# Attentions of a three-layer block on one core: values as the standing matrix, turned probabilities as the moving one, heads on column halves, no turning of outputs

## The chip, the cores and the metric

The kernel runs on one core of one Trainium2 chip. The metric is the device time of one execution in microseconds, the median of several runs. In the text PE (TensorE) multiplies matrices, DVE (VectorE) and ACT (ScalarE) do element work and read the accumulators, POOL (GpSimd) does element work on SBUF alone, and SP issues the weight loads.

## The reference, cut to what matters

Sequence 512, width 1024, float32. Two layers come first, one with a state-space scan and a differential attention, one with sliding-window attention (16 heads of 64, 2 key-value heads, window 128), then a block in which several attentions run on one projection, followed by memory attention and a feed-forward. What the change touches is how four of the attentions get from scores to outputs:

```python
def sliding_window_attention(q, k, v, sinks, slopes):
    ...
    logits = logits - sl * dist.astype(jnp.float32)
    logits = jnp.where(valid[None, :, None, None], logits, -jnp.inf)
    ...
    p = jax.nn.softmax(jnp.concatenate([logits, sink], axis=-1), axis=-1)[..., :-1]
    out = jnp.einsum('bnkgqs,bnskd->bnqkgd', p.astype(v.dtype), vv)

def odd_layer(h, w_in, b_in, sinks, w_out):
    ...
    return (o * jax.nn.silu(g)) @ w_out

def _stick_breaking(q, k, v):
        ...
        w = jnp.where(strict, jnp.exp(jax.nn.log_sigmoid(z) + suffix), 0.0)
        return jnp.einsum('bhqk,bkhd->bqhd', w.astype(v.dtype), v)

def _nsa_attention(...):
        ...
        return gb[..., 0:1] * o_cmp + gb[..., 1:2] * o_sel + gb[..., 2:3] * o_win

def _hybrid_mixer(...):
    ...
    merged = (g[:, :, 0] * (o_a.reshape(B, S, BRANCH_WIDTH) @ w_up[0]) +
    ...
```

The stick-breaking attention has 4 heads. Beside it stand a top-k attention (4 heads, an index picks 256 of the keys, then softmax and values) and `_nsa_attention` (4 heads; compressed, selected and window keys, each with its own softmax and gate).

Every output then goes, feature by feature, into a matrix product (`w_out`, `w_up`).

## The kernel before

All weights stream from memory: SP loads a 128x1024 piece `raw`, ACT cuts the high part (`cut_hi`, L224), DVE or POOL the low part (`cut_lo`, L229, which engine is set per projection by `low=`), and PE multiplies in three passes, high by high, low by high, high by low (`product`, L241 to L243). PE's order is the program order of the code: each attention is a `Part` with one generator per engine, and between the steps of an attention it takes turns from a "fill", another projection's products, so that PE has work while the softmax runs. A `run(...)` (L250) is a list of parts between two barriers of all engines.

**Sliding and branch attention.** Both are made by `attend_pairs` (L1065). A unit is a pair of heads and a tile of 128 queries; the sliding part has 32 units, the branch part 24. In step i PE computes the scores of unit i (L1139 or L1143), DVE masks them and takes the maximum (a custom instruction, L1263, twice), ACT takes the exponential with the row sums; in step i+2 PE turns the probabilities (transposes, L1166) and ACT copies them to SBUF as `pT` (L1206); in step i+3 PE multiplies (L1156) with `pT` as the standing matrix and 64 columns of values as the moving one, so the output has queries on partitions; DVE then adds the sink to the sum (L1237), takes the reciprocal (L1238), multiplies by the gate (L1240, branch only) and divides the output (L1248, or L1245 where it adds to an earlier one). Before the next unit's values PE waits for that (`out_done`). With windows of 256 keys both heads go in one group of values and one of turns; in the branch part (up to 512 keys) each head has its own.

**Outputs.** Since the next product needs features on partitions, the outputs are turned once more: by `turn_pair` (L2057) in the sliding part and in `LastTurns`, by `Turn` (L797, 24 transposes, with ACT L814 and DVE L826 cutting the high and low parts) ahead of `up`.

**Stick breaking.** For each of 4 heads PE multiplies `sb_p` tiles by values, ten matrix products of 64 columns (L2586), and DVE copies four 128x64 pieces (L2684).

**Selection.** During the branch part DVE also finds the top 256 of each index row by rounds of MAX8 and MATCH_REPLACE8 (L2805, L2807), spread over the first 21 steps (`Selection.span`).

A float32 product appears in the trace as two records, a transpose as one.

## Time and profile before

| what | value |
|---|---|
| median of 3 runs | 1581.39 us (1580.73 to 1582.72) |
| profiled execution | 1585.86 us, its span 1584.0 us |
| PE / DVE / ACT / POOL busy | 1539.8 / 841.3 / 668.0 / 265.5 us |
| sliding part, 566 to 668 us | PE 99.21 of 102 us, DVE 66.71, ACT 75.14, POOL 26.79 |
| stick breaking, 817 to 906 us | PE 88.08 of 89 us |
| branch part, 916 to 1035 us | PE 113.35 of 119 us, DVE 92.00, POOL 39.65 |

Busy times are unions of the engine's records. Records of consecutive matmuls overlap (a record lasts 0.27 to 0.40 us, while the next starts 0.1 to 0.23 us later), so the price of a group of matmuls on PE is read from start to start: from its first record to the first of what follows.

### The profile page before, as it was taken

The numbers are of one execution on the slowest core, as the hardware profiler recorded it, in microseconds if no ns is written. First come the engines' busy times: TensorE is split into PE (matmuls) and PEld (weight loads), VectorE is DVE, ScalarE is ACT, GpSimd is POOL, SyncE is SP. The second block draws the span as 40 slices with busy tenths as digits, with TensorE's granted clock in tenths as the row PEclk, the third lists the DMA queues.
The fourth block names the chain that finished last, engine by engine and source line by source line (L and its number), as shares of the span: only waits on it lengthen the run. The fifth ranks groups of instructions, "written<-read, shape, count | busy, mean of one in ns | idle before, by whom it ended". The sixth has DMA issues, their size and how long they took to land. (4 is left out here: it accounts for less than half of the span.)

```text
span 1584.0 us, 20960 instructions
## 1 busy us (share of the span) xinstructions
PE 1539.8 (97%) x7902; PEld 1272.3 (80%) x7902; DVE 841.3 (53%) x1645; ACT 668.0 (42%) x1390; POOL 265.5 (17%) x170
## 2 busy tenths in 40 slices
PE   8999999999999999998999999899999999999997
PEld 7888878888787889887888777778877888888886
DVE  3222289957834566536624476847655444444224
ACT  4222356565523367624235454553255232232122
POOL 0001044255400013200012232322322000000000
PEclk9999999999999999999999999999999999999999
DMA  5226356311322431123431211312311322322322
GB/s 213 95 94 175 104 145 162 94 47 48 120 94 80 141 92 41 42 93 97 146 96 65 80 54 54 108 41 94 103 71 41 107 93 93 107 93 94 105 94 80
DMA packets 47459, 150.21 MB, mean 95 GB/s; under 512 B 6464, under 2 KB 6848, under 8 KB 47232
## 3 DMA queue, kind: packets, MB, share of 16 engines
q1 hardware_dynamic: 41664, 136.34, 26.9%
q10 hardware_dynamic: 5696, 12.55, 2.5%
q8 instruction: 63, 1.03, 0.3%
q14 instruction: 36, 0.29, 0.1%
HBM read 128.02 MB, written 2.10 MB: 82 GB/s over the span
## 5 line engine op out<-in xcount | busy, mean ns | idle before, releaser
L224 ACT ACTIVATE cut_hi<-raw 128x1024 fp32r<-128x1024 f32 x228 | 241.5, 1059 | 561.2 <-PE ps L241 557.1
L241 PE MATMUL ps<-h_hi,cut_hi 128*128 128x512 f32 (+1 forms) x1120 | 447.8, 400 | 3.7 <-DVE h_lo L449 1.1
L243 PE MATMUL ps<-h_hi,cut_lo 128*128 128x512 f32 (+1 forms) x1120 | 436.5, 390 | 0.0
L242 PE MATMUL ps<-h_lo,cut_hi 128*128 128x512 f32 (+1 forms) x1120 | 436.1, 389 | 0.0
L229 DVE TENSOR_TENSOR cut_lo<-raw,cut_hi 128x1024 fp32r<-128x1024 f32 x170 | 211.8, 1246 | 397.2 <-ACT cut_hi L224 397.2
L241 PEld LDWEIGHTS ps<-h_hi,cut_hi 128*128 128x128 f32 x1120 | 211.3, 189 | 54.7 <-issue 13.3
L243 PEld LDWEIGHTS ps<-h_hi,cut_lo 128*128 128x128 f32 x1120 | 210.9, 188 | 45.0
L242 PEld LDWEIGHTS ps<-h_lo,cut_hi 128*128 128x128 f32 x1120 | 211.6, 189 | 37.5
L229 POOL TENSOR_TENSOR cut_lo<-raw,cut_hi 128x1024 fp32r<-128x1024 f32 x56 | 135.3, 2417 | 469.4 <-ACT cut_hi L224 469.4
L241 PE MATMUL ps<-cut_hi,h_hi 128*128 128x512 f32 (+1 forms) x304 | 117.6, 387 | 3.4 <-DVE cut_lo L229 2.9
L243 PE MATMUL ps<-cut_hi,h_lo 128*128 128x512 f32 (+1 forms) x304 | 116.7, 384 | 0.0
L242 PE MATMUL ps<-cut_lo,h_hi 128*128 128x512 f32 (+1 forms) x304 | 116.6, 384 | 0.0
L1156 PEld LDWEIGHTS ps<-arena,scr 128*128 128x128 f32 x464 | 62.5, 191 | 11.7 <-issue 4.5
L241 PEld LDWEIGHTS ps<-cut_hi,h_hi 128*128 128x128 f32 x304 | 57.1, 188 | 16.2 <-DVE cut_lo L229 3.4
L241 PE MATMUL ps<-cut_hi,ff_hi 128*128 128x512 f32 x176 | 68.6, 390 | 0.1
L242 PE MATMUL ps<-cut_lo,ff_hi 128*128 128x512 f32 x176 | 68.5, 389 | 0.0
L243 PE MATMUL ps<-cut_hi,ff_lo 128*128 128x512 f32 x176 | 68.5, 389 | 0.0
L243 PEld LDWEIGHTS ps<-cut_hi,h_lo 128*128 128x128 f32 x304 | 57.1, 188 | 11.4
L242 PEld LDWEIGHTS ps<-cut_lo,h_hi 128*128 128x128 f32 x304 | 57.1, 188 | 11.1
L1156 PE MATMUL ps<-arena,scr 128*128 128x64 f32 x464 | 61.5, 268 | 3.5 <-DVE arena L1245 1.9
L2226 POOL TENSOR_TENSOR small<-small 128x1 f32<-128x1 f32 x4 | 2.2, 548 | 360.8 <-DVE small L2238 360.8
L1206 ACT ACTIVATE scr<-scr,small 128x256 f32<-128x256 f32 (+3 forms) x112 | 56.8, 508 | 0.0
(366 smaller groups left out, 2285.2 us busy)
## 6 DMA issues: line engine op xcount, KB each, us to landing
raw<-weights SPq DMA_DIRECT2D x228, 512.0 KB, 3.3
tiles_r<-tiles_r SPq DMA_DIRECT2D x96, 128.0 KB, 2.3
scr<-scr ACTq DMA_DIRECT2D x34, 64.0 KB, 3.5
x<-x_in SPq DMA_DIRECT2D x4, 512.0 KB, 6.5
x<-x_in ACTq DMA_DIRECT2D x1, 2048.0 KB, 8.4
q_stack<-qT_lo ACTq DMA_DIRECT2D x16, 128.0 KB, 2.3
out<-x SPq DMA_DIRECT2D x4, 512.0 KB, 2.6
consts<-tables ACTq DMA_DIRECT2D x1, 1732.0 KB, 8.0
```

The costliest lines, as they stand in the source:

```text
L224: act.activation(cut_hi[:, u % CUT, :], raw[:, u % RAW, :], ACT.Copy).then_inc(hi_ready, 1)
L229: eng.tensor_tensor(cut_lo[:, u % CUT, :], raw[:, u % RAW, :], cut_hi[:, u % CUT, :].bitcast(F32), ALU.subtract).then_inc(lo_ready, 1)
L241: a = pe.matmul(out, left[0], right[0], start=start, stop=False)
L242: pe.matmul(out, left[0], right[1], start=False, stop=False)
L243: return a, pe.matmul(out, left[1], right[0], start=False, stop=stop)
L1156: last = pe.matmul(ps[:, 5, m * 64:m * 64 + 64], pT(m)[:, b * P:(b + 1) * P], u["v"][b][m], start=b == 0, stop=b == nb - 1)
L1206: last = act.activation(prob(i, m), score(i, m) if whole else prob(i, m), ACT.Exp, bias=stat(NMAX, i, m), scale=1.0 if whole else -1.0, ac ...
L2226: pool.tensor_tensor(rs[:, 32 + t:33 + t], ms[:, 32 + t:33 + t], neg_half[:, 0:1], ALU.pow)\
```

## The change

It rewrites four attentions so that the values stand on PE and the turned probabilities move past them, 128 queries at a time. A value matrix has 64 columns, so a head fills one half of the output partitions (`HALVES`), and the two heads of a pair write the two halves of one accumulator bank. The output then already has features on partitions.

- Sliding part (`SlidingWindow` in place of `attend_pairs`): the division moves ahead of the turn, as two DVE multiplications of SBUF probabilities per unit; PE's turns wait for it (`weighed`) instead of the exponential. The sink is a further column of the scores (a 128x2 DVE copy per unit), so ACT's own sink exponentials and L1237 go. `turn_pair` goes; a pair's bank is 2 or 5, and the gates of six pairs come six fill turns earlier in the plan. Two banks for turns, two `pT` buffers.
- Stick breaking: four products per head, 512, 384, 256 and 128 columns wide, and one 64x512 copy.
- Branch part (`Branches`): one group of values per unit, taken before the turns; the division and the gate in one DVE instruction per head; the two gated branches accumulate on PE, and ACT copies each finished bank (4 copies) to `o_f`. Units run by head pair, then tile, then branch. `Selection.span` is 19.
- Compressed keys: two products of 512 columns in place of four of 256. The cuts of `o_abc` (6 on ACT, 6 on DVE) stand here. The part `Turn` goes, with its 24 transposes, and `up` starts the next block.

```diff
-        class Turn(Part):
...
-                        last = pe.transpose(ps[:, k, t * P:(t + 1) * P], self.src(t, k), ident)
-                    last.then_inc(self.turned, 1)
...
-        def attend_pairs(tag, units, width, fill=None, lead=None, rest=None):
...
-                            if step >= LAG:
-                                i, u = step - LAG, units[step - LAG]
-                                nb = len(u["v"])
-                                pe.wait_ge(pT_out, ng * i + g + 1)
-                                if g == 0 and i:
-                                    pe.wait_ge(out_done, i)
-                                for m in heads_g:
-                                    for b in range(nb):
-                                        last = pe.matmul(ps[:, 5, m * 64:m * 64 + 64], pT(m)[:, b * P:(b + 1) * P],
-                                                         u["v"][b][m], start=b == 0, stop=b == nb - 1)
-                                last.then_inc(valued, 1)
-                            if 2 <= step < n + 2:
-                                i, u = step - 2, units[step - 2]
-                                pe.wait_ge(expd, i + 1)
...
-                            dve.wait_ge(expd, i + 1)
...
-                            dve.wait_ge(valued, ng * i + ng)
...
-        def turn_pair(pe, k, turned):
-            for t in range(NT):
-                last = pe.transpose(ps[:, 6 + (k + 1) % 2, t * P:(t + 1) * P], o_tok[:, t, k * P:(k + 1) * P], ident)
-            last.then_inc(turned, 1)
+        def pair_bank(k):
+            return (2, 5)[k % 2]
...
-            dve.scalar_tensor_tensor(gT[:, k, :], ps[:, 6 + (k + 1) % 2, :], 0.5, gT[:, k, :], ALU.mult, ALU.mult)\
+            dve.scalar_tensor_tensor(gT[:, k, :], ps[:, pair_bank(k), :], 0.5, gT[:, k, :], ALU.mult, ALU.mult)\
...
+        class SlidingWindow(Part):
...
+                    if step >= self.LAG:
+                        self.value(pe, step - self.LAG)
+                    if 2 <= step < self.n + 2:
+                        i = step - 2
+                        pe.wait_ge(self.weighed, i + 1)
+                        if i >= 2:
+                            pe.wait_ge(self.pT_out, i - 1)
+                        for m in range(2):
+                            for b in range(self.width(i) // P):
+                                at_t = (2 * m + b) * P
+                                last = pe.transpose(self.turn_bank(i)[:, at_t:at_t + P], self.prob(i, m)[:, b * P:(b + 1) * P],
+                                                    ident)
+                        last.then_inc(self.turned, 1)
+                    for _ in range(self.pe_turns(step, 1)):
...
+            def value(self, pe, i):
...
+                for b in range(nb):
+                    for m, r in enumerate(HALVES):
+                        at_t = (2 * m + b) * P
+                        last = pe.matmul(ps[r, pair_bank(k), t * P:(t + 1) * P], v_tok[:, first + b, kv:kv + 64],
+                                         self.pT(i)[:, at_t:at_t + P], start=b == 0, stop=b == nb - 1)
+                last.then_inc(self.valued, 1)
...
+                        dve.tensor_copy(self.sinks_beside(i), neg_sink[:, h:h + 2].unsqueeze(2))
...
+                    if 1 <= step <= self.n:
+                        i = step - 1
+                        dve.wait_ge(self.expd, i + 1)
+                        dve.reciprocal(self.stats(self.RDEN, i), self.stats(self.DEN, i)).then_inc(self.chain, 1)
+                        dve.wait_ge(self.chain, i + 1)
+                        for m in range(2):
+                            p = self.prob(i, m)[:, 0:self.width(i)]
+                            last = dve.tensor_scalar(p, p, self.stat(self.RDEN, i, m), None, ALU.mult)
...
-                if b == 4:
-                    for k in (6, 7):
-                        turn_pair(pe, k, oc_turned)
...
-                    for t in range(NT):
-                        for b in range(t + 1):
-                            last = pe.matmul(sb_out_bank(h, t), sb_p[:, b, t * P:(t + 1) * P],
-                                             tv[:, b, h * 64:(h + 1) * 64], start=b == 0, stop=b == t)
-                        last.then_inc(sb_o, 1)
+                    for b in range(NT):
+                        last = pe.matmul(sb_out_bank(h)[:, b * P:], tv[:, b, h * 64:(h + 1) * 64], sb_p[:, b, b * P:S],
+                                         start=b == 0, stop=b == NT - 1, skip_group_check=True)
+                    last.then_inc(sb_o, 1)
...
-                    for t in range(NT):
-                        dve.wait_ge(sb_o, 4 * h + 4)
-                        dve.tensor_copy(o_abc[:, t, h * 64:(h + 1) * 64], sb_out_bank(h, t)).then_inc(sb_out, 1)
+                    dve.wait_ge(sb_o, h + 1)
+                    dve.tensor_copy(o_f[HALVES[h % 2], h // 2, :], sb_out_bank(h)).then_inc(sb_out, 1)
...
-            span = 21
+            span = 19
+            banks = (0, 1, 2, 4, 5, 3)
...
+        class Branches(Part):
...
+                for b in range(nb):
+                    for m, r in enumerate(HALVES):
+                        last = pe.matmul(ps[r, 5, token_of(u)], u["v"][b], self.pT(m)[:, b * P:(b + 1) * P],
+                                         start=u["starts"] and b == 0, stop=u["stops"] and b == nb - 1, skip_group_check=True)
+                last.then_inc(self.valued, 1)
...
+                    if step - self.LAG in self.last_of:
+                        act.wait_ge(self.valued, step - self.LAG + 1)
+                        act.activation(o_f[:, units[step - self.LAG]["tile"], :], ps[:, 5, :], ACT.Copy)\
+                           .then_inc(self.drained, 1)
...
+                                last = dve.tensor_scalar(p, p, r, u["gate"][m], ALU.mult, ALU.mult)
...
+        def branch_low(dve, k):
+            dve.wait_ge(o_high, k + 1)
+            dve.tensor_tensor(o_parts[1][:, k, :], o_f[:, k, :], o_parts[0][:, k, :].bitcast(F32), ALU.subtract)\
+               .then_inc(o_low, 1)
...
-                for t in range(NT):
-                    last = pe.matmul(ps[:, 2 + t // 2, t % 2 * 256:(t % 2 + 1) * 256],
-                                     cs_turned_p[:, t * P:(t + 1) * P], vc_diag, start=True, stop=True)
-                    if t % 2:
-                        last.then_inc(cs_valued, 1)
+                for i in range(2):
+                    pe.matmul(ps[:, 2 + i, :], vc_diag[:, i * P:(i + 1) * P], cs_turned_p, start=True, stop=True)\
+                      .then_inc(cs_valued, 1)
...
+                for k in range(6):
+                    branch_low(dve, k)
...
-        run(turn_o, up, out_m, norm_q, first_query, memory, norm_f, FeedForward(),
+        run(up, out_m, norm_q, first_query, memory, norm_f, FeedForward(),
```

PE in the sliding part, two steps of it; L1139 and L1923 are scores, L1166 and L1938 turns, L1156 and L1956 values, L2057 the output turns. Before:

```order
L1139 MATMUL ps<-k_his,q_stack 128x256
L1139 MATMUL ps<-k_los,q_stack 128x256
L1139 MATMUL ps<-k_his,q_stack 128x256
L1139 MATMUL ps<-k_los,q_stack 128x256
L2057 MATMUL ps<-consts,arena 128x128 x4
L241 MATMUL ps<-h_hi,cut_hi 128x512
L242 MATMUL ps<-h_lo,cut_hi 128x512
L243 MATMUL ps<-h_hi,cut_lo 128x512
L1156 MATMUL ps<-arena,scr 128x64 x2
```

After:

```order
L1923 MATMUL ps<-k_his,q_stack 128x256
L1923 MATMUL ps<-k_los,q_stack 128x256
L1923 MATMUL ps<-k_his,q_stack 128x256
L1923 MATMUL ps<-k_los,q_stack 128x256
L241 MATMUL ps<-h_hi,cut_hi 128x512
L242 MATMUL ps<-h_lo,cut_hi 128x512
L243 MATMUL ps<-h_hi,cut_lo 128x512
L1956 MATMUL ps<-scr,arena 64x128 x2
```

The output turns are gone and nothing stands in their place; the value products keep their number and place, with the operands exchanged.

DVE in the sliding part, one step; L1263 and L2006 are the masks and maxima, L694 the fill's. Before:

```order
L1263 ISA scr,small<-ps,consts,small 128x256
L1263 ISA small 128x1
L1263 ISA scr,small<-ps,consts,small 128x256
L1263 ISA small 128x1
L694 TENSOR_SCALAR arena<-ps,cols 128x512
L1237 TENSOR_TENSOR small<-small 128x2
L1238 RECIPROCAL small<-small 128x2
L1248 TENSOR_TENSOR arena<-ps,small 128x128
```

After:

```order
L2003 COPY scr<-small 128x2
L2006 ISA scr,small<-ps,consts,small 128x256
L2006 ISA small 128x1
L2006 ISA scr,small<-ps,consts,small 128x256
L2006 ISA small 128x1
L694 TENSOR_SCALAR arena<-ps,cols 128x512
L2018 RECIPROCAL small<-small 128x2
L2022 TENSOR_SCALAR scr<-scr,small 128x128 x2
```

The division no longer reads PE's output; it works on probabilities in SBUF, and the reciprocal belongs to the unit before rather than to the one four before.

PE in the branch part where three-block units meet four-block ones; L1143 and L2871 are scores, L1166 and L2884 turns, L1156 and L2901 values, L2847 and L2711 belong to the fill. Before:

```order
L1156 MATMUL ps<-arena,scr 128x64 x3
L1166 MATMUL ps<-consts,scr 128x128 x4
L1156 MATMUL ps<-arena,scr 128x64 x3
L1166 MATMUL ps<-consts,scr 128x128 x4
L1143 MATMUL ps<-arena 128x128 x2
```

After:

```order
L2871 MATMUL ps<-arena 128x256 x2
L241 MATMUL ps<-h_hi,cut_hi 128x512
L242 MATMUL ps<-h_lo,cut_hi 128x512
L243 MATMUL ps<-h_hi,cut_lo 128x512
L2711 MATMUL ps<-consts,arena 128x32 x2
L241 MATMUL ps<-h_hi,cut_hi 128x512
L242 MATMUL ps<-h_lo,cut_hi 128x512
L243 MATMUL ps<-h_hi,cut_lo 128x512
L2901 MATMUL ps<-scr,arena 64x128 x8
L2884 MATMUL ps<-consts,scr 128x128 x4
```

Two short value groups per unit have become one of both heads, and fill products stand between the two heads' turns.

## Rows read from the trace of the kernel before

**Rows 1.** The page's first section: busy time, share, instructions by engine.
```profile
PE 1539.8 (97%) x7902; PEld 1272.3 (80%) x7902; DVE 841.3 (53%) x1645; ACT 668.0 (42%) x1390; POOL 265.5 (17%) x170
```
**Rows 2.** Windows: stretch, length, busy by engine, PE clock, DMA share, GB/s.
```profile
566.00:668.00 102.00, 99.21 (x685) 89.42 (x683) 66.71 (x250) 75.14 (x257) 26.79 (x14) 1.00 0.17 50
...
916.00:1035.00 119.00, 113.35 (x789) 88.57 (x789) 92.00 (x297) 63.42 (x155) 39.65 (x18) 1.00 0.23 76
```
**Rows 3.** Windows around the end of the sliding part, same columns.
```profile
660.00:680.00 20.00, 18.61 (x96) 15.50 (x95) 7.36 (x16) 6.58 (x13) 3.80 (x3) 0.91 0.15 52
```
**Rows 4.** PE timeline, sliding: start, duration, engine, line, operation, count, [idle before].
```profile
603.69 1.00 PE L1156 MATMUL ps<-arena,scr 128*128 128x64 f32 x8
604.53 0.61 PE L1166 MATMUL ps<-consts,scr 128*128 128x128 f32 x4
```
**Rows 5.** PE timeline, branch part: a group of four value records.
```profile
1041.72 0.55 PE L1156 MATMUL ps<-arena,scr 128*128 128x64 f32 x4
1042.11 0.39 PE L1166 MATMUL ps<-consts,scr 128*128 128x128 f32 x2
```
**Rows 6.** PE timeline, memory attention: turns, values in halves, scores.
```profile
1187.37 0.66 PE L3337 MATMUL ps<-consts,scr 128*128 128x128 f32 x4 [0.40 <-POOL scr L3389]
1187.96 0.66 PE L3348 MATMUL ps<-scr,arena 128*64 128x128 f32 x8
1188.55 0.70 PE L3324 MATMUL ps<-arena 64*128 64x256 f32 x4
```
**Rows 7.** PE timeline, sliding: one output turn and the products behind it.
```profile
596.73 0.60 PE L2057 MATMUL ps<-consts,arena 128*128 128x128 f32 x4
597.09 0.48 PE L241 MATMUL ps<-h_hi,cut_hi 128*128 128x512 f32 x1
597.40 0.39 PE L242 MATMUL ps<-h_lo,cut_hi 128*128 128x512 f32 x1
597.63 0.40 PE L243 MATMUL ps<-h_hi,cut_lo 128*128 128x512 f32 x1
```
**Rows 8.** PE timeline, stick breaking: one head's values, then one head's scores.
```profile
848.30 2.34 PE L2586 MATMUL ps<-arena 128*128 128x64 f32 x20
850.45 0.48 PE L241 MATMUL ps<-h_hi,cut_hi 128*128 128x512 f32 x1
...
856.11 2.42 PE L2561 MATMUL ps<-arena 64*128 64x512 f32 x8
858.46 0.66 PE L2564 MATMUL ps<-masks 128*128 128x128 f32 x4
```
**Rows 9.** PE timeline at the barrier behind the sliding part.
```profile
667.96 0.47 PE L241 MATMUL ps<-cut_hi,yc_hi 128*128 128x512 f32 x1 [1.39 <-PEq L250]
```
**Rows 10.** DVE groups, sliding part (busy, mean ns); then DVE and POOL timeline.
```profile
L1237 DVE TENSOR_TENSOR small<-small 128x2 f32<-128x2 f32 x32 | 11.6, 362 | 0.0
L1248 DVE TENSOR_TENSOR arena<-ps,small 128x128 f32<-128x128 f32 x32 | 9.3, 291 | 9.1 <-PE ps L1156 8.2 <-DVE small L1238 0.3
...
580.14 1.83 DVE L1237 TENSOR_TENSOR small<-small 128x2 f32<-128x2 f32 x1
...
579.58 2.38 POOL L229 TENSOR_TENSOR cut_lo<-raw,cut_hi 128x1024 fp32r<-128x1024 f32 x1 [8.84 <-ACT cut_hi L224]
```
**Rows 11.** DVE groups by form, branch part, 916 to 1036 us: busy, mean ns.
```profile
L1240 DVE TENSOR_TENSOR small<-small,arena 128x2 f32<-128x2 f32 x16 | 6.5, 407 | 0.5
...
L2811 DVE TENSOR_SCALAR arena<-arena 128x256 f32<-128x256 f32 x1 | 0.3, 293 | 0.0
```
**Rows 12.** DVE, then PE timeline where the compressed keys end and `up` begins.
```profile
1083.15 1.23 DVE L229 TENSOR_TENSOR cut_lo<-raw,cut_hi 128x1024 fp32r<-128x1024 f32 x1 [0.58 <-ACT cut_hi L224]
...
1086.79 1.88 DVE L826 SCALAR_TENSOR_TENSOR o_abc_lo<-ps,o_abc_hi 128x512 fp32r<-128x512 f32 x3 [1.62 <-ACT o_abc_hi L814]
...
1085.50 2.81 PE L797 MATMUL ps<-consts,arena 128*128 128x128 f32 x24 [0.78 <-PEq L250]
1088.13 0.51 PE L241 MATMUL ps<-o_abc_hi,cut_hi 128*128 128x512 f32 x1
```

More of the change, by code:

```diff
@@ L3068, in act @@
                 act.activation(cs_turned_p, ps[:, 4, :], ACT.Copy).then_inc(cs_pT, 1)
+                next(filler)
+                for k in range(4):
+                    branch_high(act, k)
+                for i in range(2):
+                    act.wait_ge(cs_out, i + 1)
+                    branch_high(act, 4 + i)
                 for _ in filler:
```

568 lines of the change are left out of this document (282 added, 286 removed).

## The prediction

> **What bounds the kernel now.** I read the page's busy line first: PE works 1539.8 us of a span of 1584.0, twice as long as DVE and more than twice as long as ACT [rows 1]. So time is won or lost on PE, and elsewhere only where PE comes to wait. Next the windows over the two large attentions: the sliding part has PE busy in 99.21 of its 102 us, with DVE at 66.71 and POOL at 26.79; the branch part has PE at 113.35 of 119, DVE at 92.00, POOL at 39.65 [rows 2]. The branch part is thus the one place where a second engine is near. Last the timelines of PE, in which a group's price is read from its first record to the first of the next kind. The sum below is made against the profiled execution, 1585.86 us with a span of 1584.0; the median of the runs is 1581.39, 4.5 lower, and I carry the difference over to it.
>
> **Value groups of the sliding part.** Eight old value records run from 603.69 to 604.53, 0.84 us [rows 4]; four take 0.39 [rows 5]; so a record adds about 0.11. The new form stands in the memory attention already: eight records, alternating between the two column halves, take 0.59 from 1187.96 to 1188.55. The last of them starts about 0.375 after the first (duration of the group 0.66 less one record of about 0.285). If they start in pairs, one per half, that is three steps of 0.125 per pair, where two old records take 0.22. But the neighbours pay: the four turns ahead of them take 0.59 [rows 6], where four turns among full-size tiles take 0.36 [rows 7]. Part of these 0.23 belongs to the change from the scores' tile before, so I charge half, 0.12, to entering the half-width tiles. A new group then costs 0.71 with four pairs, 0.46 with two, 0.96 with six and 1.21 with eight, an estimate. The sliding part has 8 units of one block (0.39 to 0.46) and 24 of two (0.84 to 0.71): 24 x 0.13 less 8 x 0.07, **2.5 us won**.
>
> **Value groups of the branch part.** Each unit has two old groups, one per head: at 0.11 a record, 0.17, 0.39, 0.61 and 0.84 for 1 to 4 blocks, twice 2.01 = 4.02 over the four widths. The new single groups cost 0.46 + 0.71 + 0.96 + 1.21 = 3.34. Six sets of four widths: **4.1 us won**. Over both parts that is 47.4 us of old groups against 40.8, with 232 pairs. The nearest rows below are pairs that run one record behind the other, 0.22 a pair; above, pairs at the pitch of one old record, 0.11 or a little less. I take 0.125, from the one row with this operation.
>
> The Trainium skill speaks of this swap: "TensorEngine Tiling (Array Packing)", section "Theoretical Speedup", gives up to 2x where the small dimension is at most 64. By that the 47.4 us would fall to 23.7; our row with its switches gives 40.8 (the rival "full halving" below carries its own working).
>
> **Output turns.** One `turn_pair` takes 0.36 from 596.73 to 597.09, and the product after it starts 0.31 ahead of the next, rather than 0.23: 0.44 together [rows 7]. Six go from the sliding part, **2.6 us**. The eight in `LastTurns` go as one group, 2 x 0.36 + 0.08 = **0.8 us**. Nothing takes their place in PE's order.
>
> **Stick breaking.** A head's 20 records take 2.15, from 848.30 to 850.45. The new form has eight records of 512 to 128 columns, of which only one column half works at a time. The nearest row is the same head's scores, the same eight widths: 2.35, from 856.11 to 858.46 [rows 8]. With 0.08 for the entry that is 2.43, 0.28 more, four times: **1.1 us lost**. Fewer DVE copies help nobody here.
>
> **Barrier behind the sliding part.** PE waits 1.39 there [rows 9], since DVE divides the last output and then does a bias, before the barrier. Now nothing of the attention follows the last values, and the bias can be done before. Some 0.5 of the gap stays; **0.9 won**.
>
> **Join at `up`.** The 24 transposes from 1085.50 to 1088.13 vanish, but not their time. DVE has finished the additions 0.58 before 1083.15, at 1082.57; now six cuts of 1.88/3 = 0.63 follow, 3.8, then `cut_lo`, 1.23, which makes 1087.6, then the last copy and the barrier; in the trace `cut_lo` ends at 1084.38 and PE starts 1.12 later, of which 0.37 or so is a wait [rows 12]. So `up` starts at 1088.3 to 1088.7 instead of 1088.13: **0.4 lost**. PE's own cover is gone: it idles for over 3 us, where it now turns.
>
> **The clock.** The gap of 1.39 at 667.96 is followed by a granted clock of 0.91 over 20 us [rows 3], some of these at the lower level of 1.2 GHz: 20 x 0.09 = 1.8 us. The gap at the join grows from 0.78 to over 3 and may be followed by such a stretch, 1.8 lost; the gap behind the sliding part shrinks and may give back as much. I take **0.9 lost**, with bounds of 1.8 either way.
>
> **DVE in the sliding part.** Removed are L1237, 11.6 us, and L1248, 9.3 [rows 10]. Added are two multiplications per unit, which I price with a one-input operation of 256 columns, 0.29 [rows 11], and a small copy of some 0.2: 32 x 0.78 = 25. So 66.7 becomes 70.8. There is a hidden price: at 580.14 a 128x2 addition took 1.83 us, exactly while POOL ran a `cut_lo` that started at 579.58 and took 2.38; the mean of all 32 is 0.36 [rows 10]. If every us of POOL blocked DVE, it would stand at 97.6, just what PE needs after its gain. So the sliding part does not become slower than before, and I leave this at nothing. The new wait of PE's turns on `weighed` lies a step behind the exponentials; queued behind it are that step's fill and next scores, which hide up to about a step's half.
>
> The Trainium skill bears on this too: "SBUF — State Buffer", section "Who interferes with whom", describes the ports that DVE and GpSimd share as an exclusive lock, which copies and tensor-scalar operations take in their fast modes. The new operations are of these kinds, so by that rule the change moves DVE towards the stall; the 1.83 us agrees with there being one, for an addition. The rival "DVE held" has its price from rows.
>
> **DVE in the branch part.** 92.0 now; L1240's 6.5 go [rows 11], L1245 and L1248 go too and are left uncounted; 2 x 0.29 come for each of the 19 units beside which the top-k rounds now have to finish (21 before): 11.0. That is 96.5, against 119 less PE's gain, 115. POOL is busy in a third of this time [rows 2]; a multiplication that meets its 2.4 us loses half of it on the mean, 0.4 a unit, 7.6 in all: 104, still below PE. I leave it at nothing.
>
> **Sum.** 2.5 + 4.1 + 2.6 + 0.8 - 1.1 + 0.9 - 0.4 - 0.9 = 8.5 us. The span goes from 1584.0 to 1575.5, the median from 1581.39 to **1572.9 us**.
>
> **The rivals.**
> *Full halving.* If a pair cost half of two old records with no switches, 47.4 us would become 23.7, and the gain would be 8.5 + 23.7 - 6.6 = 25.6: 1555.8 us. Against it stand the 0.59 of the turns and the 0.59 of the eight records [rows 6].
> *Branch and sliding value gains eaten by DVE's chain.* The division now lies between exponential and turn, and the rounds are pressed into 19 steps, 21/19 as many per step. If PE waits for `weighed` as long as it saves on values, 6.6 us go: 1579.5. For it speaks that DVE has only 27 us left in the branch part, against it that DVE is at most 104 of 115.
> *DVE held by POOL (slower).* If DVE is blocked for all of POOL's 39.65 x 19/21 = 36 us in the branch part, it needs 96.5 + 36 = 132 us against 115: 17 lost, 1590. It begins to cost at 18.5 us of blocking, about half of POOL's time, and eats the whole change at 27. For it: the 1.83 us above. Against it: only the multiplications that arrive during a cut are hit, and two of them stand together.
> *Pairs that do not overlap (slower).* If records of the two halves start one after the other in these places, a pair costs 0.22 instead of 0.125: 232 x 0.095 = 22 us more, 1594.9. The change breaks even at 0.125 + 8.5/232 = 0.16 a pair. Against it: 0.66 for eight records in the memory attention [rows 6], where 0.84 and more would stand.
>
> **How the numbers follow.** Forecast 0.64, with a range of its own: pairs at 0.105 give 232 x 0.02 = 4.6 more, the clock 2.7 more, so 1565.6; downwards pairs at 0.14 cost 3.5, the clock 0.9, some stalls 1: 1578. Full halving 0.06, gains eaten 0.15, DVE held 0.10, no overlap 0.05. A measurement of this kernel tells some 0.2%, 3.2 us, from no change, so 1578.2 and 1584.6 are the borders. Faster: forecast and full halving, 0.70. Same: gains eaten and a fifth of DVE held, 0.17. Slower: the rest of DVE held and no overlap, 0.13. The range goes from 1564 to 1585: full halving, no overlap and most of DVE held stay out, under 0.2.
>
> **What would show it.** In the trace after: a group of eight value records in the sliding part takes about 0.6 to its successor, and the turns behind it no more than before; in the branch part the sixteen-record group takes 1.2 or less. At the end of the sliding part PE's gap is below 0.6. At the join PE idles for 3 us or more and `up` starts no earlier than before. PE's waits in the branch part name DVE for few us; if they name DVE's multiplications for over 8 us, or single multiplications last 1 to 2 us beside POOL's cuts, DVE is held. If value records are spaced 0.1 each, pairs do not overlap. A granted clock below 0.95 in the branch part would mean gaps that I did not count.

## The result: slower by 0.2% instead of faster by 0.5%

The changed kernel takes 1585.9 us (median of 20 runs, 1582.41 to 1589.19) against 1582.19 for the kernel before beside it. The ratio is 1.0021 with an interval of 1.0014 to 1.0028: slower by about 3.3 us, where 8.5 us less were forecast. Its profiled execution has a span of 1587.3 us, against 1584.0; it is the slowest of the twenty (1589.19 us).

Lined up by the first products of each stage, the two traces differ here (us; forecast of the same places beside it). The first row holds nothing that was changed; over the twenty profiles of this case it lies between 507.0 and 511.0, which is how far single executions differ there.

| stage | before | after | difference | forecast |
|---|---|---|---|---|
| start to the fill's products ahead of the sliding part | 511.0 | 509.8 | -1.2 | 0 |
| sliding part, to the first product of `out_c` | 156.9 | 154.8 | -2.1 | -6.0 |
| `out_c` and the normalization behind it | 57.0 | 55.5 | -1.5 | -0.8 |
| projection, stick breaking, branch part to the products behind the compressed blocks | 288.2 | 289.7 | +1.5 | about -2 |
| rest of the branch part, to the memory's projection | 63.9 | 68.1 | +4.2 | about -1 |
| memory's projection and join | 11.16 | 11.14 | 0.0 | +0.4 |
| `up` | 33.4 | 35.9 | +2.5 | +0.9 (clock) |
| all behind | 462.5 | 462.4 | -0.1 | 0 |

The page of after, busy line by engine: PE works 7 us less than before [rows 1], while the span is 3.3 longer. DVE has 29.5 us more.

```profile
PE 1532.7 (97%) x7794; PEld 1233.2 (78%) x7794; DVE 870.8 (55%) x1665; ACT 660.4 (42%) x1322; POOL 266.6 (17%) x170
```

So the work did become cheaper on PE, and the groups show it. PE timeline of after: start, duration, line, count, first in the sliding part (it answers rows 4 and 6), then one head of stick breaking (rows 8), then the longest group of the branch part.

```profile
598.78 0.66 PE L1956 MATMUL ps<-scr,arena 128*64 128x128 f32 x8
599.37 0.66 PE L1938 MATMUL ps<-consts,scr 128*128 128x128 f32 x4
...
843.60 2.37 PE L2451 MATMUL ps<-arena 128*64 128x512 f32 x8
845.89 0.50 PE L241 MATMUL ps<-h_hi,cut_hi 128*128 128x512 f32 x1
...
1043.08 1.09 PE L2901 MATMUL ps<-scr,arena 128*64 128x128 f32 x16
1044.11 0.33 PE L2884 MATMUL ps<-consts,scr 128*128 128x128 f32 x1
```

Eight records take 0.59 to their successor instead of 0.84, sixteen take 1.03, a head of stick breaking 2.29 instead of 2.15. What came in is waits. PE's waits of after, in the sliding part and then from 910 to 1062, and last the longest row of before in this part (who waits, for whom, us in total, times, longest). The second list has 12.9 us in all; before it had 6.6, and the first had 1.3 for DVE:

```profile
PE ps L1938 <- DVE scr L2022: 4.8, 5, 1.6
...
PE ps L2884 <- ACT scr L2917: 7.4, 9, 1.1
PE ps L2901 <- ACT scr L2917: 1.7, 3, 0.7
PE ps L2716 <- DVE small L2729: 1.5, 1, 1.5
PE ps L241 <- POOL cut_lo L229: 1.1, 2, 0.9
PE ps L2884 <- DVE scr L2958: 0.7, 1, 0.7
PE ps L2901 <- ACT arena L2927: 0.5, 1, 0.5
...
PE ps L1166 <- ACT scr L1196: 3.2, 7, 0.7
```

So PE's waits of turns for ACT's copies of the turn bank have grown from 3.2 us to 7.4.

And the clock. Windows of after around the end of the branch part and the join (columns as in rows 2; the eighth is PE's granted clock):

```profile
1050.00:1060.00 10.00, 7.50 (x50) 5.14 (x48) 2.71 (x7) 3.75 (x9) 0.00 (x0) 0.84 0.09 36
1060.00:1070.00 10.00, 9.31 (x65) 8.52 (x66) 2.58 (x6) 4.70 (x9) 0.00 (x0) 0.50 0.01 2
1070.00:1080.00 10.00, 9.33 (x74) 8.89 (x73) 8.20 (x17) 5.42 (x11) 0.00 (x0) 0.98 0.26 81
1080.00:1090.00 10.00, 6.59 (x40) 5.27 (x39) 7.46 (x12) 5.12 (x8) 0.00 (x0) 0.88 0.26 92
1090.00:1100.00 10.00, 10.00 (x37) 8.03 (x35) 5.34 (x7) 1.10 (x2) 0.00 (x0) 0.78 0.26 91
```

From 1060 to 1070 PE ran at 1.2 GHz throughout. Full speed less the granted clock, times the length, is 1.6 + 5.0 + 0.2 + 1.2 + 2.2 = 10.2 us in these fifty; before, the same fifty were at 1.00. Not all of it is time, since PE also waits there: the two stages in which it lies grew by 4.2 and 2.5 us. That is still the largest single item, and the forecast had 0.9 for it, at the join alone.

The mean granted clock of every execution is on record. Over the twenty of the changed kernel it is 0.987 to 0.993, with a median of 0.990 (0.987 in the profiled one); over the 108 executions of the kernel before that were timed beside the experiments it is 0.991 to 0.998, with a median of 0.994. So the lower clock is no accident of the profiled execution, though its size there is at the upper end. At the same mean clock, 0.992, seven executions of the changed kernel take 1584.0 us on the mean and fourteen of the kernel before 1585.0. By this estimate the change would have won about 1 us at an equal clock: the clock makes a loss of it, and waits have eaten most of the gain that was forecast.

### The profile page after: what moved, and what is told of

It reads as the page before. It is cut to its first block and busy times, and to the rows that moved or that the text cites. A ratio compares the mean times of both kernels' runs of the same rounds, so it can differ in the third digit from the quotient of the medians.

```text
span 1587.3 us, 20505 instructions
## 1 busy us (share of the span) xinstructions
PE 1532.7 (97%) x7794; PEld 1233.2 (78%) x7794; DVE 870.8 (55%) x1665; ACT 660.4 (42%) x1322; POOL 266.6 (17%) x170
## 5 line engine op out<-in xcount | busy, mean ns | idle before, releaser
L3500 ACT ACTIVATE scr<-scr 128x512 f32<-128x512 f32 x22 | 13.9, 632 | 101.2 <-DVE scr L3515 101.1
L917 ACT ACTIVATE scr<-scr,small 128x128 f32<-128x128 f32 (+3 forms) x64 | 35.4, 555 | 36.0 <-DVE small L982 36.0
L1058 POOL TENSOR_TENSOR tiles_r<-arena,tiles_r 128x512 fp32r<-128x512 f32 x16 | 21.3, 1352 | 142.1 <-ACT tiles_r L1053 142.1
```

The costliest lines, as they stand in the source:

```text
L917: last = act.activation(prob(i, m), score(i, m) if whole else prob(i, m), ACT.Exp, bias=stat(NMAX, i, m), scale=1.0 if whole else -1.0, ac ...
L1058: pool.tensor_tensor(tiles_r[:, at_lo, :], whole[:, h, :], tiles_r[:, hi, :].bitcast(F32), ALU.subtract)\
L3500: act.activation(silu_of[:, j % 3, :], silu_of[:, j % 3, :], ACT.Silu).then_inc(self.silu, 1)
```

## Experiments

Each kernel was timed beside the kernel before on the same chip; the ratio to it stands with its 95% interval. All start from the changed kernel (ratio 1.0021) unless the text says otherwise.

### Which half: one part alone

The diff was applied in two halves: the sliding part with what belongs to it, or all the rest.

> The kernel before with the sliding part alone rewritten (with the gates and LastTurns that belong to it); stick breaking, branch part and compressed keys as before. Lining up the two traces, the rewritten sliding part lost 2.2 us of length and the product after it 1.4. Theory A (each part moves the time by its own length): 1582.2 - 3.6 = 1578.6 us, PE waiting 4 to 5 us for the multiplications of DVE in the sliding part. Rival B (the parts interact, or the lined-up difference is scatter of one execution): within 1 us of the kernel before.

> The complement: the sliding part as before, stick breaking, branch part, compressed keys and the missing turn as changed. Theory A: the whole loss sits here, 1585.9 + 3.6 = 1589.5 us, with the granted clock at half behind the end of the branch part and behind the join. Rival B (no single part is slow): between 1582 and 1586.

Measured: 1579.19 us, ratio 0.9984 (0.9975 to 0.9994), and 1589.12 us, 1.0045 (1.0033 to 1.0058). The times of theory A came in both, and in the first kernel's trace PE waits 4.8 us for the multiplications. The parts add up (-0.16% + 0.45% = 0.29%, against 0.21%), so the loss sits in stick breaking, the branch part and the join.

What theory A said of the clock did not come. The second kernel's profiled execution (1587.39 us, with a median of 1589.12) has no low clock at the end of the branch part and a short one at the join (0.93 and 0.90 from 1080 to 1100). So the two executions can be compared. PE timeline: the same value group at the end of the part in the changed kernel and in this one; then windows of this one, and one of the kernel before:

```profile
1056.68 1.46 PE L2901 MATMUL ps<-scr,arena 128*64 128x128 f32 x12 [0.58 <-ACT scr L2917]
...
1059.92 0.88 PE L2977 MATMUL ps<-scr,arena 128*64 128x128 f32 x12 [0.58 <-ACT scr L2993]
...
1050.00:1060.00 10.00, 8.28 (x47) 5.30 (x48) 4.41 (x12) 4.71 (x14) 2.52 (x3) 1.00 0.17 54
1060.00:1070.00 10.00, 7.51 (x89) 6.47 (x90) 3.48 (x9) 6.34 (x14) 0.00 (x0) 1.00 0.00 0
...
1060.00:1070.00 10.00, 8.98 (x91) 8.38 (x91) 5.44 (x13) 6.18 (x14) 0.00 (x0) 1.00 0.01 2
```

The gaps of the end are the same five (3.2 us in both kernels). But from the products behind the compressed blocks to the memory's projection this kernel takes 63.9 us, as much as the kernel before, and the changed one 68.1. So what this stage lost is the low clock; the gaps by themselves cost what the cheaper value groups gave. Eight profiled kernels leave the end of the branch part without further work on PE and with one turn bank; seven of them show a granted clock of 0.60 or less over some 10 us there, and this one does not. What decides between them no run shows.

### The clock: work that nobody needs

In the first kernel six transposes of the identity stand behind each head's turns in the two steps of the branch part that have no fill; in the second 24 stand at the end of the compressed keys.

```diff
+                        if step in (self.n, self.n + 1):
+                            for j in range(6):
+                                pe.transpose(ps[:, 0, j % 4 * P:(j % 4 + 1) * P], ident, ident)
```

```diff
+                for i in range(24):
+                    pe.transpose(ps[:, 4, i % 4 * P:(i % 4 + 1) * P], ident, ident)
```

> The changed kernel with six needless transposes behind each head's turn in the two steps of the branch part that have no fill products (24 transposes in all, about 2.6 us of PE work that nothing reads). Theory clock (PE's gaps in the tail let the granted clock fall to half from 1058 to 1070): the clock stays at 1.00 there and, though work is added, the time falls by 4 to 7 us, to 1579 to 1582. Rival chain (the tail is long because turns wait for ACT's copies, and the clock is a side effect without weight): no gain, 1585.9 to 1588.5.

> The changed kernel with 24 needless transposes at the end of the compressed keys, where PE is idle for 3.4 us before the barrier. Theory clock: up starts at the same moment but at full clock, 2 to 2.5 us faster, 1583.4 to 1584. Rival: the clock behind the join stays low because of the tail before it, or the transposes delay the barrier: 1585.9 to 1587.

Measured: 1584.82 us, 1.0014 (1.0005 to 1.0023), and 1582.52 us, 1.0002 (0.9993 to 1.0011). The second is the plain case: added work, and some 3 us won (0.19%). In its trace `up` starts after a gap of 0.78 instead of 3.41, and the clock behind it is at 1.00. PE timeline at the join of after, then of the kernel with the 24, then windows of the latter:

```profile
1089.00 0.76 PE L241 MATMUL ps<-o_abc_hi,cut_hi 128*128 128x512 f32 x1 [3.41 <-PEq L250]
1089.56 0.63 PE L242 MATMUL ps<-o_abc_lo,cut_hi 128*128 128x512 f32 x1
```

```profile
1084.35 2.79 PE L3086 MATMUL ps<-consts 128*128 128x128 f32 x24 
1087.92 0.47 PE L241 MATMUL ps<-o_abc_hi,cut_hi 128*128 128x512 f32 x1 [0.78 <-PEq L250]
...
1080.00:1090.00 10.00, 9.22 (x61) 7.74 (x60) 7.47 (x11) 4.08 (x6) 0.00 (x0) 1.00 0.33 107
1090.00:1100.00 10.00, 10.00 (x46) 8.28 (x45) 6.68 (x10) 1.66 (x2) 3.03 (x3) 1.00 0.32 106
```

A product lasts 0.63 at the lower level and 0.39 at the upper one. The first kernel missed its expectation. Its trace has the clock at 1.00 from 1050 to 1080, and the stage from the products behind the compressed blocks to the memory's projection takes 65.6 us instead of 68.1. The needless work costs nothing at that place: from the value group behind the first gap to the end of the part it is 7.5 us, as in the kernel with the sliding part as before, without transposes and at the same clock. But low stretches stand elsewhere in this execution, 0.94 and 0.89 from 1010 to 1030 and 0.68 from 1080 to 1090, where the changed kernel has 1.00 and 0.88.

### The end of the branch part and the join: useful work in the gaps

```diff
-                return min(step, self.n) * self.fill.pe_turns // self.n
+                return min(step, self.n + 2) * self.fill.pe_turns // (self.n + 2)
```

> The changed kernel with the fill products of the branch part spread over 26 steps instead of 24, so that the two steps without scores have some 10 turns of products (6 to 7 us of useful PE work). Theory tail (the end of the branch part has nothing but dependent turns, copies and values; PE's gaps there cost 3.2 us themselves and let the clock fall): the waits behind 1053 vanish, the clock stays at 1.00, and the time falls by 4 to 7 us to 1579 to 1582. Rival (DVE's rounds bound the first 19 steps, so that products taken from them open waits there): 1585 to 1588, with more PE waits before 1030.

Measured: 1578.87 us, 0.9985 (0.9976 to 0.9994): 0.36%, some 6 us, for one line, as the theory had it. Windows of this kernel:

```profile
1050.00:1060.00 10.00, 9.31 (x91) 7.58 (x90) 1.66 (x3) 3.71 (x6) 2.51 (x3) 1.00 0.17 54
1060.00:1070.00 10.00, 8.46 (x68) 7.89 (x66) 9.72 (x20) 4.87 (x11) 0.00 (x0) 1.00 0.15 52
```

From the projection ahead of stick breaking to the memory's projection its trace takes 353.1 us, the changed kernel 357.8 (289.7 + 68.1), and 353.6 with the end at full clock (289.7 + 63.9). So most of what the line gives is the clock. The waits did not all vanish: turns and values still wait 8.7 us for ACT's copies in the branch part (9.1 in the changed kernel), and the 352.0 us of the kernel before are not reached.

For the join, four `branch_high` moved to the start of the compressed keys on ACT, and three `branch_low` into gaps of DVE:

```diff
+                act.wait_ge(other_attentions.drained, 4)
+                for k in range(4):
+                    branch_high(act, k)
                 norm_kv.high(act)
...
                 next(filler)
+                for k in range(2):
+                    branch_low(dve, k)
                 next(filler)
+                branch_low(dve, 2)
...
-                for k in range(6):
+                for k in range(3, 6):
                     branch_low(dve, k)
```

> The changed kernel with four of the six high cuts of the attention outputs at the start of the compressed keys and three of the low cuts in gaps of DVE, so that three instead of six stand between the last addition and the barrier. Theory join (up waits for DVE's six cuts, and the gap lets the clock fall): PE's gap shrinks from 3.4 to 1.5 us, up starts 1.9 us earlier and at full or nearly full clock, together 2 to 4 us, 1582 to 1584. Rival (the cuts delay the chain of the compressed keys by as much): 1585.9.

Measured: 1580.52 us, 0.9994 (0.9984 to 1.0003), some 4 us, a little more than expected: the stage of memory's projection and join takes 9.3 us instead of 11.1, and `up` 33.4 instead of 35.9, at full clock.

> The changed kernel with both edits that moved the time most: fill spread over 26 steps in the branch part, and the cuts ahead of up begun earlier. Theory (two separate places, each with its own gap and its own stretch at half clock): the gains add, 1585.9 - 7.0 - 5.4 = 1573.5 us. Rival (both gains are largely the same stretch of low clock): 1577 to 1579.

Measured: 1578.24 us, 0.9977 (0.9966 to 0.9988). The sum of the two gains would be a ratio of 0.9958, known to about 0.0015 by the intervals, so the gains added only in part, at the edge of the noise. In part they were the same: with the fill alone, `up` already took 34.7 us instead of 35.9. Both places kept their gain in this kernel's profile, the join 9.3 us and `up` 33.3; but the clock is at 0.83 from 1060 to 1070, so a stretch of it was still lost there.

### The sliding part: held multiplications

Three of the four waits over 0.3 us look alike. DVE, then POOL timeline of after at one of them, then PE; last the same three for the fourth wait, the longest:

```profile
602.91 3.47 DVE L2022 TENSOR_SCALAR scr<-scr,small 128x128 f32<-128x128 f32 x2
...
602.68 2.41 POOL L229 TENSOR_TENSOR cut_lo<-raw,cut_hi 128x1024 fp32r<-128x1024 f32 x1 [7.48 <-ACT cut_hi L224]
605.03 1.27 POOL L1848 TENSOR_TENSOR yc_lo<-arena,yc_hi 128x512 fp32r<-128x512 f32 x1
...
606.44 0.44 PE L1938 MATMUL ps<-consts,scr 128*128 128x128 f32 x2 [0.93 <-DVE scr L2022]
...
567.54 1.97 DVE L2003 COPY scr<-small 128x2 f32<-128x2 f32 x1
...
567.09 2.39 POOL L229 TENSOR_TENSOR cut_lo<-raw,cut_hi 128x1024 fp32r<-128x1024 f32 x1 [60.09 <-ACT cut_hi L224]
...
570.96 0.44 PE L1938 MATMUL ps<-consts,scr 128*128 128x128 f32 x2 [1.63 <-DVE scr L2022]
```

Two multiplications that take 0.27 each elsewhere span 3.47 us, from just after the start of POOL's cut to the end of its second operation, each held by one of the two. In the fourth case no multiplication was held but the copy of the sinks, and all that follows it in DVE's order, the multiplications too, came late. The Trainium skill says as much in "SBUF — State Buffer", section "Who interferes with whom": copies and tensor-scalar operations in their two-port modes contend with GpSimd, and whoever comes second is blocked for the whole instruction of the first. The trace agrees, for the multiplications and for the 128x2 copies (1.97 us at 567.54, 0.16 in the median).

In the first kernel the fill's cuts go to DVE (`low="pool"` left out, POOL's `cut_low` taken away); in the second the turns follow a step later, and with them the fill is spread over one step more:

> The changed kernel with the fill's eight low cuts of the sliding part on DVE instead of POOL, 8 x 1.25 = 10 us more work for DVE, 19 us less for POOL. Theory lock (DVE's multiplications are held while POOL runs a cut, and PE's turns wait for them): PE's 4.8 us of waits for the multiplications fall below 1.5, no multiplication lasts over 1.4 us except beside the six small POOL operations, 1582 to 1583.5. Rival load (DVE simply has too much to do between exponential and turn): the waits grow with the 10 us, 1587 to 1591.

```diff
-            n, LAG, RING, WIDE = SW_H // 2 * NT, 3, 4, 264
+            n, LAG, RING, WIDE = SW_H // 2 * NT, 4, 4, 264
...
-                    if 2 <= step < self.n + 2:
-                        i = step - 2
+                    if 3 <= step < self.n + 3:
+                        i = step - 3
```

> The changed kernel with the turns of the sliding part one step later (three steps behind the scores instead of two, the values four), so that a multiplication of DVE that is held beside a cut of POOL has a step of slack before PE needs it. Theory slack (DVE has time enough on the mean; single multiplications held for 1 to 2 us hit PE because the turn follows too closely): PE's 4.8 us of waits for the multiplications fall below 1, the part gets 3 to 4 us shorter less about 1 for the longer end, 1582.5 to 1584. Rival (DVE is late all along): the waits stay above 3 us, 1585.9 or more.

Measured: 1587.17 us, 1.0041 (1.0027 to 1.0055), and 1581.88 us, 0.9995 (0.9984 to 1.0007). Without POOL's cuts the multiplications are indeed free: their time falls from 29.2 us to 20.7, one of 64 is over 0.7 us. But PE waits 7.0 us for them, since DVE now waits itself, 9.2 us in all, for ACT's high cuts in front of them. DVE groups of that kernel in the sliding part (busy, mean ns, idle before):

```profile
L2021 DVE TENSOR_SCALAR scr<-scr,small 128x256 f32<-128x256 f32 x48 | 15.4, 363 | 0.9
L229 DVE TENSOR_TENSOR cut_lo<-raw,cut_hi 128x1024 fp32r<-128x1024 f32 x9 | 11.0, 1225 | 9.2 <-ACT cut_hi L224 9.2
```

A step of slack does it: with the turns a step later PE's waits for the multiplications are gone, though these take 32.5 us there, more than the 29.2. The sliding part takes 151.1 us, 3.7 less than in the changed kernel and 5.8 less than before, where the forecast had 6.0. So it was one held instruction at a time that came too late, not DVE's load.

### The branch part: who holds the copies

PE's longest row of waits there is the second head's turns for ACT's copy of the first's. One of them, PE and then ACT:

```profile
975.74 0.30 PE L2884 MATMUL ps<-consts,scr 128*128 128x128 f32 x1 [1.06 <-ACT scr L2917]
...
972.94 1.06 ACT L224 ACTIVATE cut_hi<-raw 128x1024 fp32r<-128x1024 f32 x1 [3.49 <-PE ps L241]
973.91 0.58 ACT L672 ACTIVATE arena<-ps 128x512 f32<-128x512 f32 x1
974.38 1.05 ACT L2781 ACTIVATE block_hi<-arena 128x1024 fp32r<-128x1024 f32 x1
975.33 0.27 ACT L2917 ACTIVATE scr<-ps 128x128 f32<-128x128 f32 x1
```

Four edits were made around it: the odd fill turn of a step between the two heads' turns (`k // 2 if half == 0 else (k + 1) // 2`); the division on ACT as a scaled copy, DVE keeping the reciprocal; a bank of its own for the first head's turns; and, on top of that, ACT's fill pieces of a step behind its copies and exponentials.

> The changed kernel with the odd fill turn of a branch step put between the two heads' turns instead of ahead of the values. Theory cover (before, the second head's value group stood between the two turn groups and hid ACT's copy of the single turn bank; now the second turn waits for it, 7.4 us in 9 places, 3 of them in the tail): the waits of L2884 for ACT fall to 2 to 4 us, the time by 2 to 4 us, 1582 to 1584. Rival (the wait only moves ahead of the values, which need both copies of the step before, or DVE sets the pace): within 1 us of 1585.9.

Measured: 1583.42 us, 1.0016 (1.0005 to 1.0027), an interval that overlaps the changed kernel's. The first 18 steps take 103.7 us, as before and as in the changed kernel (103.9), and the waits of turns for copies 5.8 us, with 1.6 us of new ones for DVE's multiplications. The median lies in the theory's range, but neither the ratio (0.8 us less), nor the steps, nor the waits do: the rival.

> The changed kernel with the division of the branch part's probabilities on ACT (two scaled copies per unit) instead of DVE, which keeps the reciprocal and for gated units a 128x2 multiplication: some 22 us less for DVE, 18 to 20 more for ACT. In the trace the first 18 steps take 103.7 to 103.9 us whether before, after, or with fill between the turns. Theory pace (DVE's rounds and multiplications set that pace, and took the gain of the values): these steps take 99 to 101 us, the time falls by 3 to 5 us, 1581 to 1583. Rival (the chain over ACT's copies sets it): the steps take 104 or more, with longer waits of the turns for ACT, 1586 to 1590.

Measured: 1588.49 us, 1.0047 (1.0032 to 1.0062), 106.0 us for the 18 steps, and 7.8 us of waits of turns for ACT. The rival: more load on ACT makes it worse. That DVE set no pace before isn't shown by this, since ACT got what DVE lost; but PE's waits of after name DVE's multiplications here for 0.7 us only.

```diff
+            def turn_bank(self, i, m):
+                return ps[:, 4 if m else (i + 1) % 2 * 2, :]
...
+                        if i >= 3:
+                            pe.wait_ge(self.pT_out, 2 * i - 5)
...
-                        if m == 0:
+                        if m == 1:
                             for _ in range(self.pe_turns(step, 1)):
```

> The changed kernel with a bank of its own for the first head's turns in the branch part (the score bank of the unit after, free by then), so that the second head's turns no longer wait for ACT's copy of the first; the fill turns that stood between the two go behind both. Theory one bank: PE's 7.4 us of waits of turns for ACT's copies fall below 2, the first 18 steps take 100 to 101 us instead of 103.9, the time falls by 3 to 5 us, 1581 to 1583. Rival (the wait moves to the next scores or values, since the chain turn, copy, value itself is too long): the steps stay at 103 to 104 and the time within 1.5 us of 1585.9.

Measured: 1583.39 us, 1.0002 (0.9993 to 1.0012), some 3 us less, but not by the way that the theory named. The waits only moved from the turns to the scores:

```profile
PE ps L2876 <- ACT scr L2924: 6.2, 8, 1.1
PE ps L2716 <- DVE small L2729: 4.3, 1, 4.3
```

The first 18 steps take 102.8 us. Its profiled execution has the clock at 1.00 from 1030 to 1080 (though at 0.70 from 1020 to 1030), so the gain is more likely the end of the part than its pace; this is argued, not shown.

```diff
-                    for _ in range(self.turns(step)):
-                        next(filler, None)
                     for m in range(2):
                         if 2 <= step < self.n + 2:
...
+                    for _ in range(self.turns(step)):
+                        next(filler, None)
                     if step - self.LAG in self.last_of:
```

> The kernel with the bank of its own for the first head's turns (1583.4), in which ACT takes the fill's pieces of a branch step behind the step's copies and exponentials instead of ahead of them. Theory ACT's queue: PE's 6.2 us of waits of the scores for ACT's copies fall below 2, the first 18 steps take 99 to 101 us instead of 102.8, the time falls by 3 to 5 us, to 1578.5 to 1580.5. Rival (the chain of turn, copy and value is too long in itself, or the later cuts make PE wait for weights instead): the waits change their name and the time stays within 1.5 us of 1583.4.

Measured: 1587.56 us, 1.0035 (1.0024 to 1.0047). PE's waits in the branch part:

```profile
PE ps L241 <- POOL cut_lo L229: 9.9, 3, 4.9
PE ps L241 <- issue: 2.2, 1, 2.2
PE ps L241 <- ACT arena L2722: 2.2, 1, 2.2
...
PE ps L2876 <- ACT scr L2922: 0.3, 1, 0.3
```

The waits for copies are gone (0.3 us), so ACT's order is what makes them; but the same order brings the weights late, and PE waits 9.9 us for these. ACT's queue holds two things that PE needs soon. That before the change the second head's value group stood over the one and hid it, but for 3.2 us, is read from the order alone: fill turns in its place, the first of the four edits, took only 1.6 us of the 7.4 away.

### Several edits at once

> Fill over 26 steps, cuts begun earlier, and the turns of the sliding part a step later, without the division on ACT. If places add: 1578.2 less the 4.0 that the later turns gave alone, 1574 us. If the division on ACT was worth something in the kernel with four edits (1571.9), this one is slower than that by as much: 1574 means 2 us.

> The same two edits, with the division of the branch part on ACT and the turns of the sliding part a step later. If the waits of PE for DVE's multiplications are what took the gains in both attentions, 5 to 7 us below the kernel with two edits, 1567 to 1570; if DVE and ACT chains were not the limit, no faster than that.

> The kernel with those three edits and a bank of its own for the first head's turns. Theory one bank: 3 to 5 us below the kernel with three edits, 1569 to 1571, and the turns' waits for ACT below 2 us. Rival: no difference.

> The same four edits and the division of the branch part on ACT. Once the bank is no limit, DVE's load decides: theory DVE next: 1 to 3 us below the kernel with four edits. Rival (ACT, which now has 20 us more and also makes the copies, is next): as much slower.

> The fastest kernel so far (fill over 26 steps, cuts begun earlier, later turns in the sliding part, bank of its own, division on ACT; 1568.6) with the same order on ACT. Theory ACT's queue: the remaining 5.9 us of waits of the scores for ACT fall below 2 and the time to 1564 to 1566. Rival: within 1.5 us of 1568.6, or slower where the waiting exponentials hold the cuts back.

Measured: with fill to the end, earlier cuts and later turns 1572.77 us, 0.9938 (0.9927 to 0.9950); with the division on ACT besides 1571.88, 0.9941 (0.9926 to 0.9955); with the bank instead 1571.15, 0.9928 (0.9916 to 0.9941); with both 1568.62, 0.9918 (0.9904 to 0.9933). All four beat both kernels, by 0.6 to 0.8% against the one before. Division and bank are worth nothing clear each on its own; both together may give 2 to 4 us, though the medians are of 5 and 6 runs. With ACT's other order as well it is 1587.49, 1.0034 (1.0022 to 1.0045): the rival, PE again waiting for weights. The first three edits hold 13 of the 16 to 17 us. Windows of the fastest kernel:

```profile
1050.00:1060.00 10.00, 8.10 (x77) 7.65 (x76) 8.30 (x17) 8.15 (x17) 0.00 (x0) 1.00 0.09 23
1060.00:1070.00 10.00, 9.52 (x68) 8.12 (x66) 9.05 (x14) 4.30 (x7) 0.00 (x0) 1.00 0.40 137
1080.00:1090.00 10.00, 10.00 (x46) 8.29 (x45) 6.84 (x10) 2.68 (x4) 9.50 (x7) 1.00 0.36 118
```

## The prediction, point by point

- **Value groups: right in price.** 0.59 for eight records and 1.03 for sixteen, with 0.08 more from the product ahead and 0.05 more for four turns behind: 0.72 and 1.16, where 0.71 and 1.21 were forecast. Pairs cost about 0.11, nearer the lower end than 0.125, and records do run side by side. Neither "full halving" nor "pairs that do not overlap" came.
- **Output turns, barrier: right.** With a step of slack the sliding part gives 5.8 of 6.0. The gap at its end is 0.47 [rows 9 had 1.39].
- **Stick breaking: right**, 2.29 with 0.09 of entry against 2.43.
- **Sliding part, DVE: the step that failed first.** I compared sums: 97.6 us of DVE at worst against what PE needs, and left it at nothing. The sum was not exceeded, but the bound that matters is one held operation or pair against the distance from multiplication to turn. A row showed 1.83 us [rows 10]; two operations in a row can be held by two of POOL's in a row, 3.47. Cost: 3.7 of the 6.0 us, which a step of slack gave back.
- **Branch part: the step that failed second.** I priced the value groups by themselves and did not ask what they covered. Joining the two heads' groups took away what stood between the two turns, on a bank that ACT has to empty, behind fill work in ACT's queue. PE's waits in the part rose from 6.6 to 12.9 us, those of turns for copies from 3.2 to 7.4. With its end at full clock the part takes some 1 us longer than before instead of 4.1 less (289.7 + 63.9 against 288.2 + 63.9, less 0.6 for stick breaking). "Gains eaten by DVE's chain" had the right size for this part and the wrong engine: it is ACT's queue, as moving the fill pieces showed in the kernel with the second bank.
- **End of the branch part: not in the sum at all.** The fill ends with the last scores, and what follows is a chain of turn, copy and value with PE idle in between. Before, the same end was denser, since value groups alternated with turns: two gaps of 0.4 us in all against five of 3.2. The gaps alone used up what the cheaper groups gave there; the low clock, where it came, cost 4.1 us more (68.1 against 63.9). The sign that the prediction named, a granted clock below 0.95 in the branch part, came at its end (0.84, then 0.50).
- **Join: right in time, too small in clock.** `up` starts 11.1 us after the memory's projection begins, as before, where 0.4 more was forecast; the gap is 3.41. But the term for the clock was taken as half of one stretch. The whole is 2.5 us at `up` alone, and behind the sliding part nothing came back: the clock of 0.91 is gone there (1.00 from 655 to 675), but from the barrier to the normalization's end the mean is 0.94 before and after.
- **DVE held in the branch part: the sum was right.** DVE is busy 104.9 of 119 us from 911 to 1030, where 104 was forecast. The rival's sign came in both parts, single multiplications of up to 2.3 us in the sliding and 2.7 in the branch part, but not its price in the branch part: PE waited there for DVE's multiplications for 0.7 us, and giving them to ACT won nothing.
- **What stays open:** where the clock falls in executions that were not profiled (the changed kernel's spread over 7 us, the one before over 5), why it falls at the end of the branch part in seven profiled kernels and not in an eighth, and why the gains of two edits did not add in full until the sliding part was mended too.

## What to carry to other kernels

Before an operation is made cheaper or moved, ask what waited behind it: a group of matmuls that stood over a copy may be worth its length plus the wait that it covered. A normalization moved into the chain ahead of PE needs slack for its worst single instruction, not for its mean; a step of it gave 3.7 us here. A stretch at the end of a stage in which PE only waits and hops should be given fill work; if none is left, spread the fill over two more steps, which here turned 0.21% of loss into 0.15% of gain. And a profile is one execution: set its time and clock beside those of the others before its largest item is called the cause.

## What the runs showed that I had not expected

Twenty-four transposes that nobody reads, 2.8 us of PE work in a gap, made the kernel some 3 us faster. DVE's 128x2 copy was held for 2.36 us beside a POOL operation, fifteen times its usual 0.16. And the first 18 steps of the branch part took 103.7, 103.9 and 103.7 us with the value groups of before, of after, and with fill moved between the turns: a pace that a cheaper group does not touch.
